# Second attention: exps ahead of the copy of turned weights, gate tiles in pairs at nine steps

## The reference

```python
def hybrid_layer(x, cos, sin, w_in, ...):
    proj = x @ w_in                       # pool, q, k, v, xc, gate_b, gate_c, gate_logits
    o_a = multiscale_pool_mixer(u_pool, w_pool, pool_scale)
    o_b = sliding_window_gqa_sinks(q, k, v, attn_sinks)
    o_c = short_gated_conv(xc, gate_b, gate_c, conv_w)
    gates = sigmoid(gate_logits)          # [B, S, 3, D]
    merged = gates[:, :, 0] * (o_a @ w_branch_a) + gates[:, :, 1] * (o_b @ w_branch_b) \
             + gates[:, :, 2] * (o_c @ w_branch_c)
    x = layer_norm(ALPHA * x + merged @ w_o, ln1_g, ln1_b)
    up = causal_dwconv(x @ w_up, ffn_conv_w)
    ...                                   # silu gate, w_down, second layer_norm

def sliding_window_gqa_sinks(q, k, v, sinks):     # window 128, 8 query heads of 64, 2 key heads
    scores = (q . k) * 64 ** -0.5, banded over the own block of 128 keys and the one before
    probs = softmax(concat(scores, sink))[..., :-1]
    return probs @ v
```

## Time and profile before

| | |
|---|---|
| median of three runs | 2969.19 us |
| profiled execution, its own time | 2966.33 us |
| its span, first to last instruction | 2964.5 us |
| TensorE matmuls busy | 2906.9 us (98%) |
| ScalarE busy | 1595.5 us |
| VectorE busy | 1063.7 us |
| attention, first hybrid layer, first score to first branch product | 1598.81 to 1653.44 us |

### The profile page before, as it was taken

One profiled execution on the slowest core, in us unless ns is written; L12 is line 12 of the kernel. 1 busy time (PEld: TensorE's weight loads), 2 busy tenths in 40 slices (PEclk: granted clock), 3 DMA queues, 4 the chain that ended last, 5 costly groups with the idle time before them and its releaser, 6 DMA issues.

```text
span 2964.5 us, 35232 instructions
## 1 busy us (share of the span) xinstructions
PE 2906.9 (98%) x13262; PEld 2374.1 (80%) x13262; DVE 1063.7 (36%) x2146; ACT 1595.5 (54%) x2313; POOL 412.3 (14%) x477
## 2 busy tenths in 40 slices
PE   8999999999999999999999999999999999999997
PEld 6889888888887568888887788788877788788885
DVE  4534436312113773112124214423244611542234
ACT  6656656554445764444445545645555644554555
POOL 1111111111111001111110111111111011111111
PEclk9999999999999999999999999999999999999998
DMA  8666757688888327989895698788878388788876
GB/s 236 147 150 135 166 131 159 142 194 195 190 197 176 86 43 170 194 194 194 193 197 125 139 193 180 177 192 201 181 186 187 87 179 193 160 197 191 200 183 160
DMA packets 138154, 503.74 MB, mean 170 GB/s; under 512 B 15472, under 2 KB 15728, under 8 KB 137872
## 3 DMA queue, kind: packets, MB, share of 16 engines
q0 software_dynamic: 68016, 248.22, 47.1%
q1 hardware_dynamic: 69120, 251.69, 28.3%
q10 hardware_dynamic: 864, 1.72, 0.2%
HBM read 499.46 MB, written 2.10 MB: 169 GB/s over the span
## 4 chain that ended last, share of the span: by engine, by line
PE 91%; ACT 3%; DVE 3%; issue 1%; DMA 1%; DVEq 1%; ACTq 0%; POOLq 0%; POOL 0%
PE ps L1009 74%; PE ps L1027 5%; PE ps L1343 3%; PE ps L1064 1%; PE ps L1121 1%; ACT arena L887 1%; PE ps L1284 1%; PE ps L1265 1%; PE ps L1266 1%; DMA wl<-weights 1%; PE ps L1104 0%; PE ps L1210 0%; PE ps L1273 0%; DVE arena L2153 0%; ACT wl L448 0%
## 5 line engine op out<-in xcount | busy, mean ns | idle before, releaser
L444 ACT ACTIVATE wh<-raw 128x1024 fp32r<-128x1024 f32 (+1 forms) x470 | 494.9, 1053 | 1051.5 <-PE ps L1009 977.6
L1009 PE MATMUL ps<-HH,wh 128*128 128x512 f32 x2224 | 873.9, 393 | 3.0 <-DVE HL L1521 1.2
L1009 PE MATMUL ps<-HH,wl 128*128 128x512 f32 x2224 | 866.3, 390 | 0.0
L1009 PE MATMUL ps<-HL,wh 128*128 128x512 f32 x2224 | 866.0, 389 | 0.0
L428 POOL DMA_DIRECT2D wl<-weights x470 | 410.4, 873 | 2547.0 <-ACT wl L448 2546.8
L1009 PEld LDWEIGHTS ps<-HH,wh 128*128 128x128 f32 x2224 | 418.0, 188 | 95.7 <-issue 8.6
L1009 PEld LDWEIGHTS ps<-HL,wh 128*128 128x128 f32 x2224 | 418.0, 188 | 88.8 <-issue 3.1
L448 ACT ACTIVATE wl<-raw 128x1024 fp32r<-128x1024 f32 (+1 forms) x470 | 488.5, 1039 | 0.0
L1009 PEld LDWEIGHTS ps<-HH,wl 128*128 128x128 f32 x2224 | 417.8, 188 | 87.1
L1009 PE MATMUL ps<-MH,wh 128*128 128x512 f32 x1056 | 411.7, 390 | 0.7 <-DVE ML L1908 0.7
L1009 PE MATMUL ps<-MH,wl 128*128 128x512 f32 x1056 | 410.9, 389 | 0.0
(11 more groups left out here) (291 smaller groups left out, 2900.4 us busy)
## 6 DMA issues: line engine op xcount, KB each, us to landing
raw<-weights SPq DMA_DIRECT2D x472, 512.0 KB, 5.7
wl<-weights POOLq DMA_DIRECT2D x470, 512.0 KB, 7.8
XT<-x SPq DMA_DIRECT2D x4, 512.0 KB, 6.7
out<-XT SPq DMA_DIRECT2D x4, 512.0 KB, 2.7
arena<-tables POOLq DMA_DIRECT2D x1, 1024.0 KB, 12.2
arena<-table_h ACTq DMA_DIRECT2D x1, 640.0 KB, 6.1
arena<-swaps_a POOLq DMA_DIRECT2D x1, 576.0 KB, 8.3
lpar<-layers ACTq DMA_DIRECT2D x2, 218.0 KB, 7.1
```

The lines of the kernel that those rows point to most:

```text
L444: act_f(wh[:, n, 0:w], raw[:, n, 0:w], ACT.Copy)
L1009: op = mm(bank(g, t), w[:, slot, at:at + P], x[:, first + kt, :], start=(kt == 0 and w is wh and x is xh), stop=(kt == n_k - 1 and w is wl))
```

## The change

```diff
-GATE_TILES, GATE_LEAD = 32, 12
+GATE_LEAD, GATE_AT = 14, (0, 1, 2, 4, 7, 10, 13, 15, 16)
@@ def gate_tiles_at(i):
-    return 2 if i in (0, 1, 2, H_STEPS - 1) else 1 if i < H_STEPS else 0
+    return 2 if i in GATE_AT else 0
@@ ScalarE
                 for i in range(H_STEPS + 3):
+                    if i < H_STEPS:
+                        exp_heads(i, a + i)
                     if 2 <= i < H_STEPS + 2:
                         turned(i - 2)
-                    if i < H_STEPS:
-                        exp_heads(i, a + i)
                     if i == H_STEPS:
                         wait_used(act, s + 3)
                         raw_gates(0)
...
                     if i >= 3:
                         high(i - 3)
-                    if i in (2, 9):
+                    if i in (2, 8):
                         high_part(s + (SLOTS + 1 if i == 2 else SLOTS + 2))
-                    if i in (3, 10):
+                    if i in (3, 9):
                         less_high_part(s + (SLOTS + 1 if i == 3 else SLOTS + 2))
```

## The result

The changed kernel takes 2980.72 us in the median of five runs (2978.55 to 2983.44), the kernel before 2968.53 us (2967.32 to 2969.81) beside it: a ratio of 1.0044, 95% interval 1.0033 to 1.0055. It is slower by 12.2 us; 2980.6 us was forecast, in a range of 2975 to 2985.

What follows compares the result with a forecast made beforehand. The attention was taken as bound by a ring of VectorE and ScalarE, not TensorE. 0.27 + 5.13 + 0.3 = 5.7 us a layer, 11.4 us in two, on 2969.19 gave 2980.6 us, range 2975 to 2985.

Steps and rivals of the forecast that it cites:

- the ring: Attention: maxima and bias on VectorE, exps and high part on ScalarE, then low_part; a turn goes from 3.09 to 3.57 us.
- The copy in the ring: Turns 4 to 15: each copy between exps and high part adds 0.48 us wide, 0.27 narrow; 5.13 us a layer.
- Turn 2: A narrow copy leaves ScalarE's idle time and comes behind the exps, ahead of the weight stream's high_part: 0.27 us.
- the tail: Behind step 15: a later copy delays step 14's transposes and copy, so the last output comes 0.3 us later.
- The signs: Profile after: ScalarE's 6.2 us transposes wait nearly gone, its bias wait grown, VectorE's L901 wait some 5 us a layer longer.
- The gate tiles: TensorE: two more tiles ahead of score 0 fill idle time but win nothing; pairs in the turns cost 0.
- the moved pieces of the weight stream: high_part and less_high_part on ScalarE, one turn earlier, fit between high part and next exps: no cost.
- The copy outside the ring: Attention: high part waits for TensorE's output anyway, so no loss or a small gain, 2965 to 2969 us; chance 0.11.
- The late pair: Attention: a pair of gate tiles makes the copy late, 5 x 0.3 us a layer, 2984 us; chance 0.07.
- The clock: Attention: sparse turns lower TensorE's clock, 14 us more with one group of three turns a layer, 2995 us; chance 0.05.

Runs made afterwards that it cites:

- the old order: Changed kernel with the copy ahead of the exps again, so only gate tiles and weight stream are moved: 2971.20 us, ratio 1.0004 to the kernel before.
- the order alone: Kernel before with the exps put ahead of the copy and nothing else changed: 2983.53 us, ratio 1.0044 to the kernel before.
- the copy last: Changed kernel with exps, high part, then copy in turns 3 to 15, and a fourth score buffer: 2974.27 us, ratio 1.0014 to the kernel before.

## Why the prediction was right, point by point

*What bounds the attention.* Right, and shown: the ring of VectorE and ScalarE. Taking the high part out of it gave 4.4 us a layer, and doubling a copy beside the ring (kernel before) costs 0.07 us a turn on average from step 4 to 15, while doubling it in the ring costs up to 0.49.

*The copy in the ring.* Right in size: 4.65 us for the turns 4 to 14 and 0.48 for turn 15 make the 5.13 of the sum. The distance to the next instruction was the price, 0.48 and 0.27 us, not the length of 0.59.

*Turn 2 and the tail.* 0.28 us for 0.27, and 0.36 us for 0.3. The sum for an undisturbed attention was 5.7 us, and 5.78 and 5.77 were measured.

*The signs.* In the first layer ScalarE's wait for the transposes fell from 6.2 to 0.6 us, and VectorE's wait for L901 grew from 15.9 to 21.7 us (21.6 in the execution without a drop), where some 5 us more were forecast. ScalarE's wait for the bias grew from 7.2 to 20.5 us.

*The gate tiles.* Right that the lead wins nothing here: the idle time ahead of score 2 went to 0.28 us, and the first maxima come 9.24 us behind the pool mixer's product in either kernel. Right too that pairs don't make the copy late in the new order: in the undisturbed profile the turns with the pairs 7, 10 and 13 are 3.56, 3.47 and 3.57 us long (the middle one has a narrow copy, which would make 3.36, and 0.11 us more, by which one or other turn is longer in each profile, in the kernel before turn 11 with 3.20). With the old order they cost 0.6 us a layer in the profile, which the run time can't tell from nothing. What the moved pieces of the weight stream cost was not tried by itself; it is within that 0.6.

*The rivals.* The copy outside the ring fell with the order alone. The late pair fell as well, in this order; with the copy last a pair behind a late copy does cost. The clock was wrongly argued: I wrote that no pause would be longer than 1.5 us. That was reckoned from wide parts; where TensorE's part of a turn is short because of a narrow step, the pause is 1.86 us in the ring, and 2.08 in the tail of the order alone, where the turn has neither score nor tile. The mechanism came, with 2 us instead of the 14 that I gave it, since the clock was back after some 3 us and only the part of TensorE's delay that exceeds the ring's slack reaches the end.

Two of my readings on this rival were wrong. There is no pause of some 4 us ahead of the drop near the start: TensorE waits for 0.71 and 1.23 us there, and then the clock is at half, which spoke for the rival. In the second profile of the kernel before the same two pauses (0.71 and 1.22 us) left it whole. And 2.88 of 4 us is not the lowest share in the attention: around the pause of 1.64 us it is 2.36 of 4, or 0.59, nearly the 0.58 of a turn without a tile, and the clock is whole, which spoke against it. Timeline of TensorE and stretches, kernel before:

```profile
16.10 1.12 PE L1042 MATMUL ps<-cst 128*128 128x512 f32 x2 [0.71 <-ACT arena L491]
18.45 0.47 PE L1009 MATMUL ps<-HH,wh 128*128 128x512 f32 x1 [1.23 <-DVE HL L1521]
```

```profile
19.00:20.00 1.00, 1.00 (x4) 0.77 (x3) 1.00 (x2) 1.00 (x2) 0.00 (x0) 0.50 1.00 410
...
1601.00:1605.00 4.00, 2.36 (x11) 1.66 (x10) 3.74 (x14) 2.85 (x5) 0.00 (x0) 1.00 0.58 114
```

*The total.* 11.55 us from the ring and the ends and, in an execution in which both attentions have a drop, some 2 us from the clock. The 12.2 us between the medians lie between these. The forecast of 11.4 was the ring alone; it was as close as it was because a drop does not come in every execution. That 2980.6 and 2980.72 agree to a tenth is luck: the drops were not in the sum, and the forecast stood on 2969.19 us where the kernel before took 2968.53 beside the changed one.

The Trainium skill, TensorE: Matmul & The Clock Gate, section "HAM oscillation — how this bites in real kernels", tells of groups of matmuls that wait for transfers and of a clock that falls to half in each such pause. Its pauses are longer than any in these attentions, so my use of it for the sparse turns went further than it does. The traces have drops behind pauses of 1.86, 2.08 and 1.12 us all the same, and they don't come each time.

## What to carry to other kernels

In a ring of two engines ask of every instruction whether it stands between the moment an engine gets its input and the moment the other gets its output: what stands there costs its full distance in each turn, and what stands ahead of the input costs nothing until the idle time there is used up. An order that protects a critical instruction from a late one behind which it queues is worth only the lateness that the trace shows, here 0.5 us in one turn of sixteen. And look for what else is in the ring already: the largest gain here was an instruction that nobody had to wait for so soon.

## What the runs showed of the hardware that I had not expected

TensorE's granted clock fell to half for some 3 us in the attentions of the changed kernel in two of three profiled executions, with no pause above 1.86 us and a busy share of 3.24 of 6 us ahead of it; the second layer did the same as the first in each of the three. Its price at the end was 1.0 us an attention.

Neither the longest pause nor that share decides it. The execution with a whole clock had the same pause of 1.86 us and 3.25 of 6 us. In the order alone a pause of 2.08 us had a drop behind it in one layer and none in the other. And drops came behind shorter pauses: behind 1.12 us, with TensorE busy for 3.40 of 6 us, in the kernel before with copies twice, and behind 1.23 us near the start of the kernel before. What makes the difference between two executions of one kernel stays open.
